# Weight units that land in their low half's place: a six-deep ring where a three-deep ring and a six-deep ring stood

## The reference

```python
def half_step_ffn(x, g_pre, g_post, shift, scale, gate, w_gate, w_up, w_down):
    h = modulated_norm(x, g_pre, shift, scale)
    y = (jax.nn.silu(h @ w_gate) * (h @ w_up)) @ w_down
    return x + FFN_RES * gate * rms_norm(y, g_post)

m_lat = (jax.nn.silu(c) @ w_mod[i] + b_mod[i]).reshape(b, 9, 1, 1024)   # "modulation": shift, scale, gate
# layer 0: ffn (latent and context), attention + short convolution, ffn
# layer 1: ffn, Hyena long convolution by DFT, ffn
```

## Time and profile before

| | us |
|---|---|
| median of 3 runs | 1394.91 |
| lowest and highest | 1391.04, 1395.70 |
| the profiled execution's own time | 1387.58 |
| its span | 1385.9 |
| PE busy in the span | 1323.9 (96%) |
| DVE busy | 984.9 (71%) |
| ACT busy | 638.4 (46%) |

### The profile page before, as it was taken

The page is one execution under the profiler, slowest core; times in us unless marked ns, Lnnn a source line. Parts: engine busy times, 40 slices in busy tenths (PEclk is TensorE's granted clock), DMA queues, the critical chain, the costliest instruction groups (busy, mean ns, idle before and its releaser), DMA issues.

```text
span 1385.9 us, 21829 instructions
## 1 busy us (share of the span) xinstructions
PE 1323.9 (96%) x7850; PEld 1125.0 (81%) x7850; DVE 984.9 (71%) x1448; ACT 638.4 (46%) x967; POOL 118.5 (9%) x209
## 2 busy tenths in 40 slices
PE   5799999999999999999999999999999998899997
PEld 3578777887778988787898988889877887889996
DVE  4688777787776785677888577786775785775554
ACT  6533333232365565564444464444454433644443
POOL 3000011111000421011111001100000000000000
PEclk9999999999999999999999999999999999999999
DMA  9464557767655653268888648865533433656662
GB/s 359 158 206 152 191 193 270 253 232 260 219 172 170 183 155 101 93 217 314 289 296 278 201 144 310 289 229 166 168 121 111 133 120 131 245 181 188 185 186 70
DMA packets 76360, 275.12 MB, mean 199 GB/s; under 512 B 9226, under 2 KB 9781, under 8 KB 75712
## 3 DMA queue, kind: packets, MB, share of 16 engines
q1 hardware_dynamic: 52128, 187.00, 40.8%
q0 software_dynamic: 24160, 87.12, 19.1%
HBM read 273.04 MB, written 1.05 MB: 198 GB/s over the span
## 4 chain that ended last, share of the span: by engine, by line
PE 64%; DVE 13%; DMA 9%; ACT 5%; issue 4%; DVEq 0%; SPq 0%; ACTq 0%
PE gu L1629 12%; PE gu L1631 12%; PE gu L1630 12%; DMA raw<-in_wstream_dram 9%; PE acc L1690 6%; DVE wlo L984 5%; PE acc L1692 5%; PE acc L1691 5%; ACT whi L601 3%; DVE part L1001 2%; PE acc L1679 1%; PE acc L2088 1%; PE acc L1964 1%; DVE act L1174 1%; DVE z L1078 1%
## 5 line engine op out<-in xcount | busy, mean ns | idle before, releaser
L984 DVE TENSOR_TENSOR wlo<-raw,whi 128x1024 fp32r<-128x1024 f32 x350 | 426.0, 1225 | 174.3 <-ACT whi L601 172.2
L1629 PE MATMUL gu<-h_hi,whi 128*128 128x256 f32 (+1 forms) x1744 | 537.1, 308 | 9.4 <-DVE h_lo L1109 6.5
L1630 PE MATMUL gu<-h_lo,whi 128*128 128x256 f32 (+1 forms) x1744 | 530.7, 304 | 0.0
L1631 PE MATMUL gu<-h_hi,wlo 128*128 128x256 f32 (+1 forms) x1744 | 530.2, 304 | 0.0
L601 ACT ACTIVATE whi<-raw 128x1024 fp32r<-128x1024 f32 x350 | 365.3, 1051 | 177.5 <-DMA raw<-in_wstream_dram 81.6
L1629 PEld LDWEIGHTS gu<-h_hi,whi 128*128 128x128 f32 x1744 | 328.9, 189 | 40.7 <-issue 13.8
L1630 PEld LDWEIGHTS gu<-h_lo,whi 128*128 128x128 f32 x1744 | 328.7, 188 | 19.3 <-issue 2.2
L1631 PEld LDWEIGHTS gu<-h_hi,wlo 128*128 128x128 f32 x1744 | 329.5, 189 | 15.4
L1001 DVE SCALAR_TENSOR_TENSOR part<-wm,cvec,part 128x512 f32<-128x512 f32 x266 | 199.4, 750 | 6.5
L1690 PE MATMUL acc<-whi,act_hi 128*128 128x512 f32 x440 | 176.4, 401 | 9.5 <-DVE act_lo L1179 9.3
L1692 PE MATMUL acc<-wlo,act_hi 128*128 128x512 f32 x440 | 174.1, 396 | 0.0
(11 more groups left out here) (323 smaller groups left out, 1178.4 us busy)
## 6 DMA issues: line engine op xcount, KB each, us to landing
raw<-in_wstream_dram SPq DMA_DIRECT2D x350, 512.0 KB, 4.3
wm<-in_wmod_dram POOLq DMA_DIRECT2D x132, 512.0 KB, 5.4
area<-in_wmod_dram POOLq DMA_DIRECT2D x11, 512.0 KB, 20.1
z<-in_gate_rows_dram POOLq DMA_DIRECT2D x6, 512.0 KB, 7.7
gate_keep<-in_gate_rows_dram POOLq DMA_DIRECT2D x5, 512.0 KB, 7.3
area<-in_rpb_dram POOLq DMA_DIRECT2D x32, 64.0 KB, 4.7
x_lat<-in_x_in_dram SPq DMA_DIRECT2D x1, 1024.0 KB, 8.0
area<-in_ctx_in_dram SPq DMA_DIRECT2D x1, 1024.0 KB, 9.0
```

What stands on the lines that cost most here:

```text
L984: nc.vector.tensor_tensor(wlo[:, u.base % RING, :], raw[:, u.base % RAW, :], whi[:, u.base % RING, :].bitcast(F32), ALU.subtract).then_inc ...
L1629: nc.tensor.matmul(out_, w_hi, x_hi, start=start, stop=False, skip_group_check=True)
L1630: nc.tensor.matmul(out_, w_hi, x_lo, start=False, stop=False, skip_group_check=True)
L1631: return nc.tensor.matmul(out_, w_lo, x_hi, start=False, stop=stop, skip_group_check=True)
```

## The change

- The tensor `raw` goes. `raw` is now another name for `wlo` (fp32 beside fp32r): a unit lands in its low half's place, u mod 6, and DVE subtracts in place.
- SP issues the load of unit u when PE is done with unit u-6 (`pe_done`) and no longer waits for `lo_done`. There are six landing semaphores instead of three. ACT's wait for `pe_done` ahead of a split goes, since the load has waited for it.
- ACT and DVE split unit u+k+4 in step k (LEAD = 4) where they split u+k+6. The places between the stages follow: held units are 2 and 3 instead of 4 and 5; units 4 and 5 of the first FFN are split in its first turn; in the Hyena output projection splits of units 4 to 7 stand ahead of `mixed_hi` instead of behind it.
- `job_sum` of FFNs 2 to 4 moves from the end of a turn to behind unit 0 of the next turn. Turn 1 is written out for that, so the loops begin at turn 2.
- The chunks at the start get places by a table, with two spare tensors; loads of units 2 to 5 wait until PE has used the last chunk of their place.

```diff
-RAW = 3
+LEAD = 4
-LOOPS = [{3: 6}, {1: 6}, {1: 4}, {3: 10}]
+LOOPS = [{3: 6}, {2: 6}, {2: 4}, {3: 10}]
+CHUNK_SLOT = [2, 3, 4, 5, 2, 3, 4, 5, 2, 3, None, 4, 5, None, 4, 5]
...
-        raw = sb("raw", [P, RAW, UNIT])
+        spare_hi = sb("spare_hi", [P, UNIT], F32R)
+        spare_lo = sb("spare_lo", [P, UNIT], F32R)
         whi = sb("whi", [P, RING, UNIT], F32R)
-        wlo = sb("wlo", [P, RING, UNIT], F32R)
+        raw, wlo = both("wlo", [P, RING, UNIT])
...
             for u in range(2):
                 load(u, u)
             sp.wait_ge(ahead_landed[AHEAD_CHUNKS - 1], 16)
-            load(2, 2)
-            for u in range(RAW, RING):
-                sp.wait_ge(lo_done, u - RAW + 1)
+            for u in range(2, RING):
+                sp.wait_ge(ahead_used, last_chunk(u) + 1)
                 load(u, u)
             with sp.Fori(1, turns) as i:
                 for k in range(RING):
-                    sp.wait_ge(lo_done, i * RING + (k - RAW + 1))
+                    sp.wait_ge(pe_done, i * RING + (k - RING + 1))
                     load(i * RING + k, k)
...
-            def split_hi(u, phase, first=False):
+            def split_hi(u, phase):
                 if isinstance(u, int):
-                    a.wait_ge(landed[u % RAW], 16 * (u // RAW + 1))
+                    a.wait_ge(landed[u % RING], 16 * (u // RING + 1))
                 else:
-                    a.wait_ge(landed[base % RAW], i * 32 + 16 * (base // RAW + 1))
-                if not first:
-                    a.wait_ge(pe_done, at_unit(u, -RING + 1))
-                nc.scalar.activation(whi[:, phase % RING, :], raw[:, phase % RAW, :], ACT.Copy).then_inc(hi_done, 1)
+                    a.wait_ge(landed[u.base % RING], u.i * 16 + 16 * (u.base // RING + 1))
+                nc.scalar.activation(whi[:, phase % RING, :], raw[:, phase % RING, :], ACT.Copy).then_inc(hi_done, 1)
...
-                        split(u.plus(k + RING))
+                        split(u.plus(k + LEAD))
...
-            for u in range(4, RING):
-                split_hi(u, u, first=True)
...
             for c in range(4, KT):
+                for u in {4: (4, 5), 5: (6,), 6: (7,)}.get(c, ()):
+                    split(Unit(U_HYO + u))
                 mixed_hi(c)
-                split(Unit(U_HYO + c - 4 + RING))
...
-            def ffn_turn(u, n, na, job, xs, first=False, wait_h=None, last=False, between={}):
+            def ffn_turn(u, n, na, before, xs, first=False, wait_h=None, last=False, between={}):
...
                         column_unit(uk, gu[:, s, (k % 2) * T:(k % 2) * T + T], xs)
+                        if k == 0 and before is not None:
+                            job_sum(*before)
...
-                    if k == 5 and job is not None:
-                        job_sum(*job, first)
```

More of the change, by code:

```diff
@@ L397, in bias_part @@
             return (both_hi, both_lo)[part_][:, 2 * h - 12:2 * h - 10, LAT, :]
-        landed = [sem(f"unit_landed{i}") for i in range(RAW)]
+        landed = [sem(f"unit_landed{i}") for i in range(RING)]
         hi_done, lo_done, pe_done = sem("hi_done"), sem("lo_done"), sem("pe_done")
@@ L819, in _ @@
                     context_his(ft + 2, ft % 2, Unit(U_CD + ft + 2))
-                split(Unit(U_CD + ft + RING))
+                split(Unit(U_CD + ft + LEAD))
                 if ft in beside:
@@ L858, in _ @@
                 take_out(idx)
-                split(Unit(U_AB + idx + RING))
+                split(Unit(U_AB + idx + LEAD))
                 if idx in beside:
@@ L873, in _ @@
             load_table(ACT.Exp)
-            split(Unit(U_AB + 20 + RING))
+            split(Unit(U_AB + 20 + LEAD))
             exps(0)
-            split(Unit(U_AB + 21 + RING))
+            split(Unit(U_AB + 21 + LEAD))
             exps(1)
@@ L879, in _ @@
             bias_his(5)
-            split(Unit(U_AB + 22 + RING))
+            split(Unit(U_AB + 22 + LEAD))
             a.wait_ge(pe_done, U_AB + 24)
@@ L883, in _ @@
                 nc.scalar.activation(v_n[:, t, :], acc[:, t, :], ACT.Copy).then_inc(proj_out, 1)
-            split(Unit(U_AB + 23 + RING))
+            split(Unit(U_AB + 23 + LEAD))
             for h in range(HEADS):
@@ L932, in _ @@
             square(10, 1)
-            split(Unit(U_HY + 4))
+            split(Unit(U_HY + 2))
             spectrum_out(0)
@@ L937, in _ @@
             spectrum_out(1)
-            split(Unit(U_HY + 5))
+            split(Unit(U_HY + 3))
             h_his(11)
@@ L953, in _ @@
                                      scale=sm[:, S_SHORT + 24 + j:S_SHORT + 25 + j]).then_inc(hy_act, 1)
[L954 removed]
+                split(Unit(U_HY + idx + LEAD))
                 if idx < 7:
@@ L1328, in _ @@
             second_los(1)
-            for u in range(4, RING):
-                split(Unit(u))
             nc.vector.tensor_copy(turn_r[:, :], turn[:, :]).then_inc(turn_made, 1)
@@ L1600, in _ @@
                 taps(idx)
-                split(Unit(U_HY + idx + RING))
+                split(Unit(U_HY + idx + LEAD))
                 if idx == 10:
@@ L1610, in _ @@
             for c in range(4, KT):
+                for u in {4: (4, 5), 5: (6,), 6: (7,)}.get(c, ()):
+                    split(Unit(U_HYO + u))
                 inverse_out(c)
-                split(Unit(U_HYO + c - 4 + RING))
             for c in (4, 5):
-                split(Unit(U_HYO + c + RING))
-            norms(12, (U_F4 + 4, U_F4 + 5))
+                split(Unit(U_HYO + c + LEAD))
+            norms(12, (U_F4 + 2, U_F4 + 3))
             ffn(3)
```

59 lines of the change are left out of this document (31 added, 28 removed).

## The result

The changed kernel takes 1373.34 us (median of 4 runs, 1371.79 to 1373.65) against 1395.31 us for the kernel before beside it (4 runs): ratio 0.9855, 95% interval 0.982 to 0.989. Run again later (run 7) it came to 1374.96 us against 1393.54, ratio 0.9861 (0.9837 to 0.9884).

The account below looks back on a forecast made before the run. PE was taken as the bound, losing time to the three-deep raw ring and the turn-end sum. Wins of 3.3, 2.3, 0.2 (FFNs 2 to 4) and 2.5 (start) make 8.3, less 0.8: 1394.9 - 7.5 = 1387.4 us; 8-in-10 range 1379 to 1397.

Parts of the forecast that it names:

- What bounds the kernel: FFNs 2 to 4: three-deep raw ring and the sum at turn's end cause PE excess of 7.5, 4.9 and 2.2 us.
- The offset: Whole kernel: shown median 7.3 us above the profiled execution, carried over to put the forecast on the median's scale.
- Loads by `pe_done`: Steady job turns: a landing may take 7.8 us before it costs anything, so the ring's wait was taken as gone.
- what would show it: Signs: job turns at 17.4 to 17.6 us, ACT's landing waits gone in steady turns, no PE wait for `total_lo`.
- Gate jobs: Turns behind gate jobs: two more DVE steps (1.4 us), so 1.3, 1.1 and 0.7 us of excess left in FFNs 2, 3, 4.
- First turns: First turns of FFNs 2 to 4: unit 6's late split adds PE waits of 2.9, 1.5 and 1.3 us.
- The start: Chunks and first FFN's first turns: +0.5 - 1.0 - 1.5 - 0.5 = -2.5 us; bounds 0 and -3.3.
- 0.8 off for small waits: Whole kernel: 0.8 us taken off the 8.3 us won, for small waits that couldn't be placed, leaving 7.5.
- Rival 1: Job turns: DVE becomes the bound and they stay at 18.0 us; -1.5 us, 1393.4; chance 0.24.
- rival 2: Job turns: unit u+6 lands later than 7.8 us, silu waits every turn; +11 us, 1406; chance 0.11.
- rival 3: First turns: SP's units land within 4.6 us and the three waits go; -13.2 us, 1381.7; chance 0.12.
- rival 4: Splits: DVE's in-place subtraction is slower, over 3 us a job turn, over 30 us in all; chance 0.02.

Follow-up runs that it names:

- run 7: The changed kernel once more, unchanged, against the kernel before; 1374.96 us (4 runs), ratio 0.9861.
- Runs 5: The kernel before with modulation-weight loads in the loops of the first three FFNs cut to a sixteenth of their bytes; 1382.39 us, ratio 0.9919.
- 14: The kernel before with splits four ahead, later column sums, three landing places kept, and light modulation loads; 1377.21 us, ratio 0.9886.
- Run 4: The kernel before with two raw landing places instead of three; 1533.89 us, ratio 1.1024.
- run 13: The kernel before with splits four ahead and later column sums, three landing places and loads released by `lo_done` kept; 1387.21 us, ratio 0.9963.
- run 15: The changed kernel with each load in the loop released one unit later, five units ahead instead of six; 1405.48 us, ratio 1.008.
- run 1: The kernel before once more, unchanged; 1391.51 us, ratio 1.000, profiled span 1389.6 us.
- 11: The kernel before with the start's split order, the first turns' split behind step 3's silu, and light modulation loads together; 1378.08 us, ratio 0.9915.
- run 3: The changed kernel with the column sums back at the end of the turn; 1376.47 us, ratio 0.9889.
- Run 8: The changed kernel with step 2's split moved behind step 3's silu in the first turn of FFNs 2 to 4; 1369.41 us, ratio 0.9825.
- run 10: The kernel before with only the start's order changed, units 4 and 5 split in the first turn instead of ahead of it; 1396.04 us, ratio 1.0036.
- 2: The kernel before with only the column sums moved behind the next turn's first unit; 1392.47 us, ratio 0.9991.
- 9: The kernel before with step 2's split moved behind step 3's silu in the first turn of FFNs 2 to 4; 1393.62 us, ratio 1.0017.

## Why the forecast went wrong, step by step

**What bounds the kernel: right.** The excess of the job turns lay in the three-deep ring and silu behind a held split. Runs 5 and 14 show it most directly: with short landings three places give turns of 17.4 us. Run 4 shows the ring bare, run 13 that the splits' distance does not cure it, run 15 what a shorter time for the landing costs.

**The offset: the largest miss.** The forecast says "The median shown is 7.3 us above that execution" and carries the 7.3 over unchanged. The changed kernel's median is 0.3 us *under* its profiled execution. Those 7.3 us were no constant. The profiled execution lies 4.7 us below the mean of the 77 runs of run 1 and its neighbours (4 of them are as short), with a clock above all of theirs; the three runs of the median shown lie 2.7 us above that mean. Both are the chance of few executions. The changed kernel varies little: its 8 runs lie within 4.1 us, against 15 us for the 77. So of the gap of 14.1 us between forecast and result, 7.6 stand here. Run 1 shows the variation of the kernel before. That the change ends it by taking away late landings that reach PE, and the lower clock behind such waits, fits the smaller spread of the kernels with short landings (5.2 us in runs 5 and 11, 7.9 in run 14), but how the 7.6 divide between waits, clock and the chance of three runs stays open.

**Loads by `pe_done`: right in mechanism.** The turns took 17.4 us, as forecast, and landings of units issued in 640 to 780 us were 7.2 us at most, under the 7.8. Run 15 bears out that this margin was needed. But ACT's waits for landings did not go, as "what would show it" had said; ACT had 2 us in hand behind them.

**Gate jobs: wrong.** The forecast left 1.3, 1.1 and 0.7 us in the excess (3.1 in all) for them; by the forecast's own ideals 2.2, 2.0 and 0.6 us of excess remain in FFNs 2, 3 and 4, 4.8 in all, and 3.7 of them are the first turns' waits, which leaves 1.1. The changed kernel has no wait of PE at a gate turn where the earlier trace rows shows 1.04. Second silu to second silu, that turn took 19.1 us before, 18.0 with light loads (run 5), 17.9 in run 3 with the sum still at the end of the turn, and 17.5 in the changed kernel and in run 14. So that turn lost 1.1 us through late landings (before against run 5), and 0.4 through the sum's place (run 3 against the changed kernel).

**First turns: right in kind, 2.0 us too long.** Forecast 2.9, 1.5 and 1.3 us; measured 1.86, 1.54 and 0.30. Unit 6 was asked for at 614.49 us and split at 621.28, and PE went on at 624.98, the 3.7 us behind it that had been taken from before. The landing took 6.8 us where 7.5 had been taken. Run 8 took these waits away.

The page of the Trainium skill named in the forecast would have had no waits there. Here two units of the SP queue, issued in 613.5 to 617 us beside POOL's gate rows (8.9 us) and weight part (9.0 us), landed in 6.8 and 8.7 us. The estimate worked out from the page's two figures should have read 4.4 us, not 4.6 (2 us, and 0.524 MB at half of 436 GB/s), figures that the page gives for transfers issued from GpSimd; it was worked out for a single unit, and both landings are above it, as the forecast took it.

**The start: right in kind, and the match of size is luck.** Forecast 2.5, measured 2.2 at the first wait, 4.6 at the first FFN's last silu (368.05 against 363.41), and 2.5 at the start of FFN 2, where 2.1 are given back. Of each of these 1.0 is the chance of the two executions that stands already at 31 us, so some 1.5 came by the start of FFN 2. PE's wait of 1.50 us at 87 us is gone, as forecast. Run 13 ties the gain to the splits' distance, run 10 shows that order alone does not do it.

**Not forecast:** in the norm ahead of FFN 4, PE's wait for `diag` shrank from 2.44 to 1.13 us (the kernel before, then the changed one):

```profile
1183.01 3.84 PE L1679 MATMUL acc<-diag,x_lat 128*128 128x128 f32 x32 [2.44 <-DVE diag L1092]
```

```profile
1170.51 3.84 PE L1685 MATMUL acc<-diag,x_lat 128*128 128x128 f32 x32 [1.13 <-DVE diag L1099]
```

The splits' distance does this: the wait is 1.13 us in runs 13 and 14 too, which keep three landing places, and 2.2 to 2.8 in runs 1, 2, 5, 9 and 11, which split six ahead. That it comes through a held split which no longer stands ahead of ACT's squares is argued from the order of the code. And "0.8 off for small waits" had no ground.

Summed against the profile: 14.0 - 7.5 = 6.5 us. From the first turns come 2.0 (of 5.7 forecast 3.7 stood), from the gate turns 2.0 (of 3.1 left in the excess 1.1 stood), from the Hyena stage with its norms 1.6, and 0.8 from what was taken off without ground; 0.1 is rounding.

**Rivals.** Rival 1 (DVE bound) is refuted by 17.4 us a turn; rival 2 (late landings stop every turn) did not come in the change, but run 15, with one unit's step less, is close to it, at +30 us over the changed kernel; rival 3's price (-13.2, on the profile 14.0) was met for other reasons, since in the first turns landings of 6.8 and 8.7 us were not within 4.6; rival 4 is refuted by 1222 ns.

## What to carry to other kernels

Where an in-order engine waits for a transfer ahead of work that the critical engine needs, don't sum its waits: look how often that work finds the engine ready, and give each transfer the time of its slow landings, not of its mean ones. A load released by the engine that sets the pace can't be held up by one that is itself late; here that was changed together with the number of places, so its own worth is not shown. And before a forecast is put on the scale of a median, compare the profiled execution with the spread of the runs: an offset that varies is partly chance, and partly what a change can take away.

## What the runs showed of the hardware beyond that

A wait of PE can cost more than its length. In FFN 2's first turn the 12 matmuls of the down unit behind the wait stand 0.23 us apart after the changed kernel's wait of 1.86 us, and the next unit begins 2.91 us after the first of them. After run 1's wait of 2.92 us most of them stand 0.43 us apart, the pace of the lower of the two levels of 1.2 and 2.4 GHz, and what follows begins 4.45 us after the first:

```profile
627.45 0.50 PE L1690 MATMUL acc<-whi,act_hi 128*128 128x512 f32 x1 [2.92 <-DVE act_lo L1179]
...
628.47 0.63 PE L1690 MATMUL acc<-whi,act_hi 128*128 128x512 f32 x1
628.90 0.63 PE L1691 MATMUL acc<-whi,act_lo 128*128 128x512 f32 x1
```

So that wait cost 1.5 us more than its 2.92. In run 14, behind the wait of 3.61 us, already the first matmul takes 0.79 us, and the 12 take 5.24 us, 2.3 more than in the changed kernel; the same start is seen after 3.54 and 4.54 us in runs 5 and 15:

```profile
628.15 0.80 PE L1690 MATMUL acc<-whi,act_hi 128*128 128x512 f32 x1 [3.54 <-DVE act_lo L1179]
```

```profile
642.80 0.79 PE L1696 MATMUL acc<-whi,act_hi 128*128 128x512 f32 x1 [4.54 <-DVE act_lo L1186]
```

The length of the wait alone does not decide how soon the lower level comes: after 3.55 us in run 10 the first matmul still took 0.50. The stretches of 620 to 640 and 625 to 630 us in run 14 were granted 0.83 and 0.50 of full speed in the mean:

```profile
620.00:640.00 20.00, 16.39 (x94) 14.19 (x94) 11.85 (x18) 7.63 (x11) 1.60 (x3) 0.83 0.73 256
625.00:630.00 5.00, 3.39 (x8) 2.71 (x9) 4.96 (x10) 3.33 (x5) 1.07 (x2) 0.50 0.54 191
```

The transfers of the SP queue, issued in 640 to 780 us of the kernel before, take 5.0 us in the median beside full modulation loads and 4.1 beside light ones, with the worst at 7.1 and 4.8: the other queue moves the tail more than the middle. That the tail is what this kernel paid for fits the one microsecond that the ring leaves for a late landing, and is argued.
